# Hybrid streaming encoder layer on one core: input projection and attention without a barrier between them, v projected last by token tiles

## The reference, cut to what matters

```python
h = x @ w_in                       # [2176, 1024] @ [1024, 3584], cut into seven parts of 512
u_a = gelu(u); v_a = layernorm(gelu(va)); y_A = (W_s-mix of v_a + b_s) * u_a * silu(z_a)   # 128-token chunks, 4 groups
q, k, v_b; y_B = band_attention(q, k, v_b, relative bias) * silu(z_b)                # 8 heads of 64, up to 640 keys
y = layernorm(ALPHA * x + [y_A ; y_B] @ w_out)                                       # w_out [1024, 1024]
```

## Time and profile before

| | |
|---|---|
| median of 3 runs | 1177.2 us (1177.04 to 1177.67) |
| the profiled execution, its own time | 1179.38 us |
| its span | 1177.7 us |
| busy in the span: PE, PEld, DVE, ACT, POOL | 95%, 82%, 41%, 28%, 19% |
| mean granted TensorE clock | 0.978 |

### The profile page before, as it was taken

One profiled execution on the slowest core, in us unless ns is written; L12 is line 12 of the kernel. 1 busy time (PEld: TensorE's weight loads), 2 busy tenths in 40 slices (PEclk: granted clock), 3 DMA queues, 4 the chain that ended last, 5 costly groups with the idle time before them and its releaser, 6 DMA issues. The chain is left out here.

```text
span 1177.7 us, 18220 instructions
## 1 busy us (share of the span) xinstructions
PE 1116.0 (95%) x7040; PEld 962.9 (82%) x7040; DVE 488.2 (41%) x972; ACT 334.1 (28%) x689; POOL 219.0 (19%) x163
## 2 busy tenths in 40 slices
PE   6999999999999999999999983899999999999996
PEld 5999999999899999999999972566777778888775
DVE  4400212022222322223232224567666677776764
ACT  4411211111111111111111111234555455545540
POOL 0000000000000001000001014534333334433343
PEclk9999999999999999999999995799999999999999
DMA  8561111011432343333333339653434333334211
GB/s 270 185 191 63 54 38 56 27 65 49 134 134 84 122 143 97 121 123 127 105 122 132 117 103 325 185 148 122 120 121 122 114 103 99 109 121 143 69 37 72
DMA packets 135097, 137.52 MB, mean 117 GB/s; under 512 B 7656, under 2 KB 110720, under 8 KB 135040
## 3 DMA queue, kind: packets, MB, share of 16 engines
q1 hardware_dynamic: 130720, 121.01, 32.3%
q10 hardware_dynamic: 4320, 15.73, 4.1%
HBM read 87.41 MB, written 52.45 MB: 119 GB/s over the span
## 5 line engine op out<-in xcount | busy, mean ns | idle before, releaser
L578 PE MATMUL bank<-xh,wh 128*128 128x384 f32 (+1 forms) x1120 | 404.8, 361 | 9.9 <-DVE xl L464 8.5
L578 PE MATMUL bank<-xh,wl 128*128 128x384 f32 (+1 forms) x1120 | 401.0, 358 | 0.0
L578 PE MATMUL bank<-xl,wh 128*128 128x384 f32 (+1 forms) x1120 | 400.5, 358 | 0.0
L578 PEld LDWEIGHTS bank<-xh,wh 128*128 128x128 f32 x1120 | 211.1, 188 | 28.1 <-issue 9.6
L578 PEld LDWEIGHTS bank<-xh,wl 128*128 128x128 f32 x1120 | 210.8, 188 | 18.2
L578 PEld LDWEIGHTS bank<-xl,wh 128*128 128x128 f32 x1120 | 211.1, 188 | 17.5
L1043 ACT ACTIVATE pt<-pt_ps 128x512 f32<-128x512 f32 (+1 forms) x168 | 82.2, 524 | 181.7 <-PE pt_ps L1288 178.6
L1345 PE MATMUL out_ps<-wo_h,yh 128*128 128x512 f32 x264 | 114.9, 435 | 4.7 <-DVE yl L1237 1.9
L1051 ACT ACTIVATE prob<-prob,low 128x640 f32<-128x640 f32 (+3 forms) x136 | 101.1, 745 | 24.4 <-DVE low L1116 24.4
L1345 PE MATMUL out_ps<-wo_l,yh 128*128 128x512 f32 x264 | 105.3, 399 | 0.0
L1345 PE MATMUL out_ps<-wo_h,yl 128*128 128x512 f32 x264 | 104.5, 396 | 0.0
(11 more groups left out here) (117 smaller groups left out, 969.0 us busy)
## 6 DMA issues: line engine op xcount, KB each, us to landing
raw<-w_all ACTq DMA_DIRECT2D x30, 512.0 KB, 3.4
par<-x SPq DMA_DIRECT2D x17, 512.0 KB, 3.9
q<-s_q SPq DMA_DIRECT2D x16, 512.0 KB, 4.1
k<-s_k SPq DMA_DIRECT2D x16, 512.0 KB, 5.5
y_out<-par SPq DMA_DIRECT2D x15, 512.0 KB, 2.6
big<-s_va SPq DMA_DIRECT2D x17, 256.0 KB, 3.3
big<-s_gate SPq DMA_DIRECT2D x17, 256.0 KB, 3.5
s_y<-big SPq DMA_DIRECT2D x16, 256.0 KB, 2.4
```

Source lines behind the costliest of these rows:

```text
L578: last = nc.tensor.matmul(bank[c][:, 0:width], w[s][:, kc, :], xx[:, kc, t0:t0 + width], start=kc == 0 and a == 0, stop=kc == KC - 1 and a ...
```

## The change

**One block.** The two functions become one, with SBUF addresses given by hand, so that attention's buffers lie where a chunk of x was. The order of the groups is now z0 and z1 (chunk by chunk, while x comes in), va, u and za alternating, k and q alternating, z2 and z3, and v last. All instructions of all engines are written out, where the projection before had loops on the engines.

**va and v by token tiles.** For these the 128-token tile of x is stationary and the weights of all four groups move (512 columns, four pieces of 128 that lie 8 KB apart), so the result lies tokens by channels and no transposes are needed (17 tiles each, 24 matmuls a tile). va is normalised and mixed right behind its tile, and the mixed result goes to DRAM (s_mix) until u is there. 9 of the 17 v tiles run before attention. The other 8 take the place of the quarters in steps 0 to 15.

**Splits in place.** x and weights are loaded where their low part will be, and w_out too (8 pieces: 4 from step 10, 4 from step 16).

**Schedule.** Every one of now 84 steps has a quarter: steps 0 to 15 of v, steps 16 to 83 of the output. Output tile n starts at START[n] = 16 + 4n, and its split stands at START[n] - 1, which is the step in which the second half of tile n-1 ends. The streams follow tiles 4 to 11. Step 72 turns and weighs the last unit, so steps 73 to 83 have quarters only. The halves of the last three output tiles alternate between two banks. Attention's gated result goes through DRAM (s_y) together with the gMLP's. Cut to its core:

```diff
+GROUPS = [("z", 0), ("z", 1)] + [("va", g) for g in range(GRP)]
+GROUPS += [(kind, g) for g in range(GRP) for kind in ("u", "za")]
+GROUPS += [(kind, g) for g in range(GRP) for kind in ("k", "q")]
+GROUPS += [("z", 2), ("z", 3)] + [("v", g) for g in range(GRP)]
+NGROUPS = len(GROUPS)
+SINGLE = range(6, 24)
+V_FIRST = 24
+SLOT = [4, None, 0, 1, 2, 3, 4, 0, 1, 2, 3, 4, 0, 1, 2, 3, 4, 0, 1, 2, 0, 1, 3, 4, 0, 1, 2, 3]
+LOADED_BEFORE = [SLOT[:i].count(s) for i, s in enumerate(SLOT)]
+LOADS_IN = {i: [i + 2] for i in SINGLE}
+LOADS_IN.update({6: [7, 8], 22: [24, 25, 26], 23: [27]})
+SPLITS_IN = {(i, 2): [i + 1] for i in SINGLE}
+SPLITS_IN.update({(23, 0): [24], (23, 1): [25], (23, 2): [26], (23, 3): [27]})
+V_EARLY = 9
...
+            b = event[1] % 4 if event[0] == "va" else 1 + 2 * (event[1] % 2)
...
+STREAM_AFTER = 4
...
+V_STEPS = 2 * (TILES - V_EARLY)
+STEPS = V_STEPS + 4 * TILES
+ORDER = [*range(PTILES - 1), PTILES, PTILES - 1]
+START = [V_STEPS + 4 * n for n in range(TILES)]
+SPLIT = [s - 1 for s in START]
+GATED = [gate_step(t) for t in range(PTILES)] + [PLACE["stream", SB - 1, None] + 3]
+Y_LOAD = [max(START[max(n - 2, 0)] + 1 - 7 * (n < 2), GATED[ORDER[n]] + 1) for n in range(TILES)]
+X_LOAD = [V_STEPS + 1, V_STEPS + 1] + [START[n - 2] + 7 for n in range(2, TILES)]
...
+        x_at = [2 * KC * 4 * t0 for t0, _ in CHUNKS]
+        xh = [at(f"xh{c}", x_at[c], [KC, n], f32r) for c, (_, n) in enumerate(CHUNKS)]
+        xl = [at(f"xl{c}", x_at[c] + 4 * KC * n, [KC, n], f32r) for c, (_, n) in enumerate(CHUNKS)]
+        x_raw = [at(f"x_raw{c}", x_at[c] + 4 * KC * n, [KC, n]) for c, (_, n) in enumerate(CHUNKS)]
+        ring_at = 2 * KC * 4 * T
+        ring = at("ring", ring_at, [5, 2, KC, P], f32r)
+        raw = [at(f"raw{s}", ring_at + 8192 * s + 4096, [KC, P]) for s in range(5)]
...
-            k, h = half // 2, half % 2
-            return s_ps[0][:, 0:512] if k >= TILES - 1 and h == 1 else out_ps[:]
+            step = START[half // 2] + 2 * (half % 2)
+            return s_ps[0][:, 0:512] if step > NU and half % 2 else out_ps[:]
+        def out_free(half):
+            step = START[half // 2] + 2 * (half % 2)
+            return half - 1 if step > NU + 2 else half
...
+            for m in range(PIECES * NCH):
+                c, held = piece(m)
+                t0, n = CHUNKS[c]
+                sp.dma_start(x_raw[c][held], x_t[:, held[1], t0:t0 + n]).then_inc(x_loaded[m], 16)
...
+                    sp.wait_ge(proj_done, DONE["v", 7])
+                    sp.wait_ge(rel_stored, 16 * (2 + HEADS))
+                    near = skewed(s_skew, slice(0, HEADS), P, WIN - P, WIN)[:, :, WIN - NEAR:WIN]
+                    sp.dma_start(bias[:, 2 * NEAR:].rearrange("p (h j) -> p h j", h=HEADS), near).then_inc(bias_loaded, 16)
+                    load_z(0)
+                    load_z(1)
+                    sp.wait_ge(u_mixed, GRP * NCH)
+                    load_v(0)
+                    load_v(1)
...
+                if step == 10:
+                    sp.wait_ge(proj_done, DONE["v", 13])
+                    for j in range(4):
+                        load_wo(j)
+                if step == V_STEPS:
+                    sp.wait_ge(proj_done, DONE["v", TILES - 1])
+                    for j in range(4, 8):
+                        load_wo(j)
+                    load_keys(0)
...
+            pool.wait_ge(proj_done, DONE["v", 7])
...
+                if step < V_STEPS and step % 2 == 1:
+                    copy_v(V_EARLY + step // 2)
+                if step in SPLIT:
+                    y_high_part(SPLIT.index(step))
...
+                if step >= V_STEPS and (step - V_STEPS) % 2 == 1:
+                    n, h = divmod((step - V_STEPS) // 2, 2)
...
                     if h == 1:
                         moments(n)
                         if n >= POOL_TILES:
                             finish(n)
-                for n in range(TILES):
-                    if SPLIT[n] == step:
-                        dve.wait_ge(y_high, n + 1)
-                        src = yr[ORDER[n] % 2] if ORDER[n] < PTILES else ysamp[:]
-                        nc.vector.tensor_tensor(yl[n % 2][:], src, yh[n % 2][:].bitcast(f32),
-                                                ALU.subtract).then_inc(y_split, 1)
+                if step in SPLIT:
+                    n = SPLIT.index(step)
+                    dve.wait_ge(y_high, n + 1)
+                    nc.vector.tensor_tensor(yl[n % 2][:], yr[n % 2][:], yh[n % 2][:].bitcast(f32),
+                                            ALU.subtract).then_inc(y_split, 1)
...
+            def project_tile(kind, t, k0, k1):
+                b, used = BANK[kind, t]
+                c = max(n for n in range(NCH) if CHUNKS[n][0] <= t * P)
+                cols = slice(t * P - CHUNKS[c][0], t * P - CHUNKS[c][0] + P)
+                if k0 == 0:
+                    if t == 0:
+                        pe.wait_ge(w_ready, 6 if kind == "va" else NGROUPS)
+                    if used:
+                        pe.wait_ge(evac[b], used)
+                out = bank[b].rearrange("p (g t) -> p g t", g=GRP)
+                for kc in range(k0, k1):
+                    for a, (xx, side) in enumerate(((xh[c], 0), (xh[c], 1), (xl[c], 0))):
+                        last = nc.tensor.matmul(out, xx[:, kc, cols], ring[:, 0:GRP, side, kc, :],
+                                                start=kc == 0 and a == 0, stop=kc == KC - 1 and a == 2)
+                if k1 == KC:
+                    last.then_inc(proj_done, 1)
...
+            for c in range(NCH):
+                for i in range(2):
+                    project_chunk(i, c)
+            for t in range(TILES):
+                project_tile("va", t, 0, KC // 2)
+                if t >= 2:
+                    mix(t - 2)
+                project_tile("va", t, KC // 2, KC)
+            for i in SINGLE:
+                for c in range(NCH):
+                    project_chunk(i, c)
+                    if i == SINGLE[0] and c < 2:
+                        mix(TILES - 2 + c)
+            for t in range(V_EARLY):
+                project_tile("v", t, 0, KC)
...
+            def quarter(step, part):
+                if step < V_STEPS:
+                    k0 = 4 * (step % 2) + 2 * part
+                    project_tile("v", V_EARLY + step // 2, k0, k0 + 2)
+                else:
+                    n, j = divmod(step - V_STEPS, 4)
+                    k0 = 4 * (j % 2) + 2 * part
+                    project_out(n, j // 2, k0, k0 + 2)
             for step in range(STEPS):
                 if step < NU:
                     if UNITS[step][0] == "stream":
                         stream_scores(step)
                     else:
                         scores(step)
                 groups = turned_groups(step - 1) if 1 <= step <= NU else 0
                 for e in range(min(2, groups)):
                     turn(step - 1, e)
                 if 2 <= step < NU + 2 and UNITS[step - 2][0] == "stream":
                     turn_back(UNITS[step - 2][1])
-                if step in QUARTERS:
-                    n, h, part = QUARTERS[step]
-                    project(n, h, 4 * part, 4 * part + 2)
+                quarter(step, 0)
                 if groups > 2:
                     turn(step - 1, 2)
-                if step in QUARTERS:
-                    project(n, h, 4 * part + 2, 4 * part + 4)
+                quarter(step, 1)
```

More of the change, by code:

```diff
@@ new lines, with banks, stores @@
+EVENTS = projections()
+DONE = {event: n + 1 for n, event in enumerate(EVENTS)}
+def banks():
+    place, used, chunk = {}, [0] * NCH, 0
+    for event in EVENTS:
+        if event[0] == "chunk":
+            b, chunk = chunk % NCH, chunk + 1
+        else:
+            b = event[1] % 4 if event[0] == "va" else 1 + 2 * (event[1] % 2)
+        place[event] = (b, used[b])
+        used[b] += 1
+    return place, used
+BANK, BANK_USED = banks()
+def stores():
+    place, count, turn = {}, [0] * 4, 0
+    for event in EVENTS:
+        if event[0] == "chunk":
+            kind = GROUPS[event[1]][0]
+            slots = [(turn + j) % 4 for j in range({"u": 0, "q": 2, "k": 2}.get(kind, 1))]
+            turn += len(slots)
+        elif event[0] == "va":
+            slots = [2 + event[1] % 2] + ([0] if event[1] == TILES - 1 else [])
+            turn = 0
+        else:
+            slots = [2 + event[1] % 2]
+        place[event] = [(s, count[s]) for s in slots]
+        for s in slots:
+            count[s] += 1
+    return place, count
@@ L645, in key_tiles, with counted @@
+STAGED, STORES = stores()
+OPENING_STORES = [len(range(s, 2 * NCH, 4)) for s in range(4)]
+STORES_BEFORE_V = [STORES[0], STORES[1], STAGED["v", 0][0][1], STAGED["v", 1][0][1]]
+def counted(kinds):
+    out = {}
+    for event in EVENTS:
+        if event[0] == "chunk" and GROUPS[event[1]][0] in kinds:
+            out[event] = len(out) + 1
+    return out
+HANDED = counted(("z", "za", "q", "k"))
+U_COUNT = counted(("u",))
+ZA_COUNT = counted(("za",))
```

(45 more changed lines are left out.)

1388 lines of the change are left out of this document (591 added, 797 removed).

## The result

The changed kernel takes 1142.9 us (median of 4 runs, 1141.5 to 1145.2) against 1177.4 us for the kernel before on the same chip: a ratio of 0.971, 95% interval 0.969 to 0.9725. In a second session it was 1142.2 us and 0.9695 (0.968 to 0.971). The profiled execution took 1142.3 us with a span of 1140.5.

The account below looks back on a forecast made before the run. PE bounds the kernel except around the barrier. Projection to 640, waits 2, steps 428, late splits 12, tail 51.4 and end 7.7 gave a 1141 us span; 1 more for w_out and s_y made 1142, range 1130 to 1155.

Parts of the forecast that it names:

- Projection: Stretch before attention: 692.2 us falls to 631 by fewer transposes and eight v tiles leaving; v tile 8 ends about 640.
- waits at the start of attention: After v tile 8: bias load about level with PE's cover, first turn waits for a softmax; 2 us, between 0 and 5.
- rival (d): Projection of va and v: moving operand in four pieces 8 KB apart slows matmuls; 35 us at 19%, up to 185; chance 0.04.
- Steps 0 to 15: First attention steps with quarters of v: four each at 4.0, 4.6, 5.8 and up to full length, 79 us.
- (c): First attention steps: late bias, idle PE and half clock replace the barrier; 20 to 79 us more, 1162 to 1221; chance 0.06.
- (e): Start of attention: tiles 4 to 8 merely cover loads, the barrier in disguise; given nothing beyond (c).
- Steps 16 to 71: Attention with output quarters: 48 steps of 6.44 us, 309, and eight stream steps of 5 us, 40.
- the late split: Output tiles 1 to 13: PE waits about 1.0 us each for yl behind DVE's residual work; 12 us, between 5 and 40.
- 0 to 3: From step 16: w_out's second half, loaded and split piece by piece, is hidden by little; 1 us taken with s_y's DRAM way.
- Tail: Steps 72 to 83: short steps no longer hide DVE's chain; waits 1.8, 0.9, 3.5, 6.8 and clock 3, sum 51.4 us.
- Rival (b): Output tiles: yl falls behind POOL's passes, 3.39 us; 1167, or 1191 with the full lock; chance 0.20, of which 0.03 lock.
- Rival (a): Output steps and tail: late splits cost nothing in steps, little in the tail, as DVE gets ahead; 1125 us; chance 0.14.

Follow-up runs that it names:

- the combined kernel: Changed kernel with yl ahead of the residual, x of the first two output tiles issued first at step 16, and the stream's copies moved off POOL's passes: 1106.7 us.
- the run with yl first: Changed kernel with DVE's low part of y taken ahead of the residual, statistics and final pass of the tile before: 1119.0 us.
- the repeat: The changed kernel once more, nothing edited, in the session of the follow-up runs: 1142.2 us.
- two other kernels: Changed kernel with x of the first two output tiles issued first at step 16, 1137.5 us; changed kernel with the stream's copies at earlier steps, 1136.6 us.
- the run without cover: Changed kernel with all 17 v tiles projected ahead of attention and none in steps 0 to 15, loads of step 0 still early: 1172.1 us.

## Why the prediction was right, and where it was not

The time was right within 1 us (1142 against 1142.9), and the main mechanisms were right. But two misses of about 15 us were made up for by terms that were priced too high, so that the total is this close is partly luck. The span's terms can be set side by side.

- **Projection.** Step 0 starts at 638.6 us, forecast about 641. The stretch takes 629.1 us (631), from a start that is 1 us later. The sum behind the 631 has an error: 692.2 less 7.0, 7.5, 1.9 and 43.5 and plus 0.9 is 633, so the terms as listed were 4 us above the measured stretch, not 2, and the forecast should have read 1144. Half of that can be seen: PE was idle for 3.0 us in the old stretch, the longest of it 1.6 us for a tile of va that came back from DRAM, and is for 0.8 in the new one; I had not counted these waits. The rest stays open. The 2 us for waits at the start of attention came as two of 0.7 us, at 643 and 695 us. 215 distances between v's matmuls take 48.77 us, 0.227 each: rival (d) falls. The transposes were priced at 14.5 us, and 15.1 us is what they cost when put back.
- **Steps 0 to 15** take 78.0 us (79), at clock 1.00. Rivals (c) and (e) fall: PE waits for no DMA there. Taking the cover away and putting the barrier back costs 45 us together; I had said "about 40" for the two.
- **Steps 16 to 71** take 365.8 us; I had 309 + 40 for the work, 12 for the late split and 1 for w_o. The work was over-priced by 5 to 6 us: freed of nearly all waits, the same stretch is 344.4 us in the combined kernel, 1.3 us of it waits for the delayed residual. The term "12 us" measured 4.6 us of idle time and, by the steps' lengths once the copies are out of the way, about 8 us for thirteen waits. The mechanism was right, its size too large by a third. Most of that third is the length of yl itself: I had taken 1.46 us, and it takes 1.17, which is 3.8 us in thirteen tiles (my estimate).
- **What failed** is the path that I took as "0 to 3", with w_out's split as the only late thing: the x of the first tile, issued behind it, was late by 5.65 us, and with the clock step 18 lost 8.5. I had counted the queue's loads for w_out and y but not the one issued behind them. Also missing were the stream's copies behind POOL's pass, 6.4 us of stands. I had looked for that collision at yl, and it was at another operation of DVE. These two misses, some 15 us, were made up for by the over-priced work (6), late split (4), w_o (1) and 4 us ahead of them; the right total rests partly on that.
- **Tail.** 50.4 us for 51.4: waits of 1.25, 0.85, 3.0 and 6.4 us where I had 1.8, 0.9, 3.5 and 6.8, and 2.1 us for the clock where I had 3 (47 distances in 13.0 us instead of 10.9).
- **Rival (b).** yl takes 1.17 to 1.23 us all 17 times, never 3.39: in the new order it starts ahead of POOL's passes. The 3.39 us were no rarity. In the kernel before, yl began behind POOL's multiplication by gain seven times, and took 3.39 each time; it cost PE next to nothing (0.5 us idle in all from 960 to 1133.8 us), since the quarter stood four steps later. In the run with yl first it came second twice, in the tail, and did wait (2.91 and 3.35 us); that run still was the faster.
- **Rival (a)**, 1125 us because DVE gets ahead and the splits cost nothing, did not come about: PE waited for yl in the steps and in the tail. Its price was near: the run with both halves a step earlier takes 1126.9 us.

So where did the gain go? Putting back cover, barrier and transposes costs 29.9 + 15.4 + 15.1 = 60.4 us, if they add up, and the change brought 35. The other 25 us were given back later: 4.7 by the late x, 5.6 by the copies and 23.2 by the order of the late split, each measured alone, 33.5 in all. These overlap in part with waits that the kernel before had too (it lost 6.0 us to stream steps and 1.9 to yl), so how the 25 us divide is worked out and not shown by a run.

## What to carry to other kernels

When the cover moves, list every transfer that is issued in the first steps in the order of its queue, and look at the last, not only the largest. Where an engine's program is in fixed order, put what the bounding engine waits for next ahead of what only closes the tile before: here that one move gave 2%. And look for small operations that a long pass of another engine holds up, here copies of 0.19 us behind passes of 2.4 us and more; the step in which they stand decides, not their length.

## What the runs showed of the hardware

**A stand costs more than its length.** After stands of PE of 2.8 us and more the granted clock was often lower for the next stretch: 0.77 over step 18 with its stand of 5.1, 0.63 for 8.6 us after one of 2.84, 0.78 for 11.2 us after one of 6.4. Not always: after another of 2.86 it stayed at 1.00, and after one of 3.0 in the tail it was 1.00 in the repeat and 0.86 and 0.87 in two other kernels. The full clock is 2.4 GHz, and a mean between 0.5 and 1 over a window is a mixture of its two levels. No such fall followed a single wait of 1.4 us or less where PE was otherwise full; in the run without cover, with waits of about 0.7 us in nearly every step, three of 1.6 to 2.5 and 25% idle time, the clock was 0.70.

**A pass of POOL stops some operations of DVE until it ends.** In the run with yl first, at the end of tile 15:

```profile
1096.06 2.39 POOL L728 TENSOR_TENSOR r<-r,gain 128x1024 f32<-128x1024 f32 x1
1096.19 3.35 DVE L1110 TENSOR_TENSOR yl<-yr,yh 128x1024 fp32r<-128x1024 f32 x1
1098.53 3.26 POOL L730 TENSOR_TENSOR r<-r,offset 128x1024 f32<-128x1024 f32 x1
```

POOL's pass ends at 1098.45, yl at 1099.54, 1.09 us later: it ran only then. POOL's next pass takes 3.26 us instead of 2.39, as if it had waited for yl in turn. In the kernel before, all seven yl that began inside the pass by gain ended 1.1 us behind it too. The Trainium skill ("SBUF — State Buffer", section "SBUF: two separate sides") says that whichever operation starts first has the shared port for its whole instruction; these rows agree, and so does the copy at 782.22 us.

Beside POOL's pass by a scalar it was otherwise. In the changed kernel the copies at 781.13 and 781.24 us, begun in the last microsecond of that pass (778.07 to 782.10), ended with it. In the run with yl first the second copy, begun with 1.2 us of the pass left, was not held, and the third, begun with 1.0 left, was:

```profile
778.79 3.79 POOL L725 TENSOR_SCALAR r<-r,mv_o,rstd_o 128x1024 f32<-128x1024 f32 x1
...
781.36 0.18 DVE L1043 COPY qd<-qs 64x64 f32<-64x64 f32 x1
781.57 1.05 DVE L1044 COPY qd<-qs 64x64 f32<-64x64 f32 x1
```

Nor is the 1.46 us of yl an exception: all eight yl of the kernel before that began inside this pass took 1.22 to 1.46 us. The rule of the Trainium skill for the whole instruction does not fit these rows, as the prediction said; no run here tells why.
